# Router of a tiled decoder step: once per four tiles in four column groups instead of once per tile

## The chip, the cores and the metric

The kernel runs on one core of a Trainium2 chip. The metric is the device time of one execution in microseconds (us). The core has a matrix engine (TensorE, PE in the rows, with its weight loads as PEld), a vector engine (DVE), an activation engine (ACT), GpSimd (POOL) and a sync engine (SP), which here only issues DMAs, in order. The engines are tied together by semaphores: an instruction waits until a counter has reached a value, and everything behind it on its engine waits with it.

## What is computed

The reference is one step of a hybrid decoder layer for 2048 prompt tokens and 64 sample tokens of width 1024. Cut to what matters here:

```python
x = x + g1 * (concat(pool_out, ssm_out) @ w_out)
h2 = modulate(rmsnorm(x, norm2_g), sh2, sc2)
lg1 = h2 @ rw1 + rb1                       # 4 columns: the expert groups
lg2 = einsum('td,gde->tge', h2, rw2) + rb2 # 16 columns: the experts
# top-1 group, top-2 experts inside it, gates, then the expert MLPs, gated residual, final norm
```

The ssm half of the mix is g * sigmoid(g @ glu_w + glu_b) (the "GLU"). The router is the product of h2 with the 20 columns of rw1 and rw2.

## The kernel before

The program has the stages front, middle, routing, experts and final_norm, with a barrier between them. The change lies in the second part of `middle`, a loop over 17 tiles: 16 of 128 prompt tokens and a last one (LAST = 16) of 64 sample tokens.

For tile t, in the order that each engine's own list gives:

- **PE**: `product(t, 0)` and `product(t, 1)`, the two column halves of the ssm half of the output projection, each 12 matmuls of 512 columns into `psO[:, t % 2]`; between them `turn(t - 2)`, eight transposes of the rows h2 of tile t-2 into `psH`; behind them `route(t - 2)`, the router; then `gate(t + 5)`, 12 matmuls of the GLU for one of its 20 pieces (`LEAD` is 5, `GLUS` 20; four pieces make one block of four tiles; pieces 16 to 19 are those of the sample tokens and are 64 columns wide).
- **ACT**: sigmoid of the gate, in every fourth tile `g_split` (the high part of the next GLU block), the square sum of the row norm, its square root, `gated_hi`, and `turned(t - 1)`, which copies `psH` to `h2T`.
- **DVE**: `residual(t)` (three passes over 1024 columns: L1706, L1708, L1710), `gated(t + 5)` (L1689), in every fourth tile `g_split`, `mean`, `normed(t)` (L1720, L1721, and L1726, which writes h2), `gated_lo` (L1697), at t = 2 also `scale_rows(1)`, and `logits(t - 2)` (L1731), which adds the bias `rb` to `psR` and writes `lg`.
- **SP**: `store(t)` (x2 to acc_d, L1191, and h2 to h2_d, L1193), then `tile_load(t + 2)` (L1181, L1185: the rows of x and of the pooling half `part_d`), and in tiles 3 and 7 `g_load`, four DMAs of the next GLU block.

Ahead of the loop SP issues, in this order: the broadcast rows g1, a2, sh2 and norm2_g, five DMAs of the router weight `rw` (L1255, L1257), two of the bias `rb` (L1259, L1260), three of the sample tokens' rows, and `g_load(2)` (L1173). The buffers of this part lie over buffers of the first part: `rw`, `rb` and `ss` over `mp_hi`, `h2T` over `ev0`, `n2` over `mraw`.

What ties the router to the rest is this:

```python
def route(t):
    ...
        pe.wait_ge(s["lg_done"], t)      # logits(t - 1) is done on DVE: psR is free
    pe.wait_ge(s["h_ev"], t + 1)         # turned(t) is done on ACT
```

PE's `route(t - 2)` of tile t thus waits for DVE's `logits(t - 3)`, and that is the last thing DVE does for tile t-1. `product(t, 0)` waits for the first pass of `residual(t - 2)`, `gate(n)` for the sigmoid of piece n-1, DVE's `gated(n)` for the sigmoid of piece n, `residual(t)` for `product(t, 1)` and for the landing of `part`.

## Time and profile before

| | |
|---|---|
| median of 3 runs | 1302.78 us (1300.69 to 1307.26) |
| profiled execution | 1300.7 us, its span 1299.0 us |
| PE busy | 1086.8 us, 84% |
| DVE busy | 761.1 us, 59% |
| ACT busy | 512.3 us, 39% |
| mean granted TensorE clock | 0.907 of full speed |

Busy time is the sum over all stages; it doesn't say which engine sets the end in one of them. The rows below are from the span's own clock, which begins with the first instruction. In a timeline row the first number is the start, the second how long the (merged) entry took; in brackets stands the idle time ahead of it and what ended it. A matmul's duration includes its passage through the array, so successive starts, not durations, tell the pace. An fp32 matmul stands as two instructions; the products and gates, in fp32r, as one.

### The profile page before, as it was taken

The numbers are of one execution on the slowest core, as the hardware profiler recorded it, in microseconds if no ns is written. First come the engines' busy times: TensorE is split into PE (matmuls) and PEld (weight loads), VectorE is DVE, ScalarE is ACT, GpSimd is POOL, SyncE is SP. The second block draws the span as 40 slices with busy tenths as digits, with TensorE's granted clock in tenths as the row PEclk, the third lists the DMA queues.
The fourth block names the chain that finished last, engine by engine and source line by source line (L and its number), as shares of the span: only waits on it lengthen the run. The fifth ranks groups of instructions, "written<-read, shape, count | busy, mean of one in ns | idle before, by whom it ended". The sixth has DMA issues, their size and how long they took to land. (4 is left out here: it accounts for less than half of the span.)

```text
span 1299.0 us, 18067 instructions
## 1 busy us (share of the span) xinstructions
PE 1086.8 (84%) x5419; PEld 832.6 (64%) x5420; DVE 761.1 (59%) x1248; ACT 512.3 (39%) x759; POOL 257.1 (20%) x316
## 2 busy tenths in 40 slices
PE   4599999998488989989999824999999999999900
PEld 2266766765265668777788613777787777787700
DVE  2745566630589934475767667465566655555326
ACT  2523333311343225344444321455556545444315
POOL 0035344351140000000000001133233323233200
PEclk9699999998689989988898856999999999999955
DMA  9814646483774458465355453678789778765469
GB/s 295 305 38 123 193 116 196 122 288 98 213 112 131 137 180 259 127 232 162 144 185 195 146 195 120 204 210 224 219 272 284 213 216 223 225 155 108 74 202 394
DMA packets 175876, 244.75 MB, mean 188 GB/s; under 512 B 70903, under 2 KB 131015, under 8 KB 174743
## 3 DMA queue, kind: packets, MB, share of 16 engines
q1 hardware_dynamic: 151049, 180.32, 43.4%
q0 software_dynamic: 12528, 45.62, 15.4%
q10 hardware_dynamic: 12246, 18.14, 4.1%
q8 instruction: 29, 0.48, 0.1%
q14 instruction: 24, 0.20, 0.0%
HBM read 167.80 MB, written 75.84 MB: 188 GB/s over the span
## 5 line engine op out<-in xcount | busy, mean ns | idle before, releaser
L120 PE MATMUL experts_psGU<-weights_we_hi,experts_x_hi 128*128 (+1 forms) x344 | 144.7, 421 | 9.0 <-DVE experts_x_lo L2292 6.9
L121 PE MATMUL experts_psGU<-weights_we_hi,experts_x_lo 128*128 (+1 forms) x344 | 137.5, 400 | 0.0
L122 PE MATMUL experts_psGU<-weights_we_lo,experts_x_hi 128*128 (+1 forms) x344 | 137.5, 400 | 0.0
L120 PE MATMUL front_psM<-front_hT_hi,front_w_hi 128*128 128x512 f32 x256 | 105.7, 413 | 0.0
L2188 POOL DMA_INDIRECT acc_d<-experts_o_sb,experts_to_col x43 | 71.4, 1660 | 149.6 <-issue 64.4
L121 PE MATMUL front_psM<-front_hT_hi,front_w_lo 128*128 128x512 f32 x256 | 100.5, 393 | 0.0
L122 PE MATMUL front_psM<-front_hT_lo,front_w_hi 128*128 128x512 f32 x256 | 100.3, 392 | 0.0
L120 PEld LDWEIGHTS experts_psGU<-weights_we_hi,experts_x_hi 128*128 128x128 f32 x344 | 65.6, 191 | 34.9 <-issue 22.8
L2292 DVE TENSOR_TENSOR experts_x_lo<-experts_psX,experts_x_hi 128x1024 fp32r<-128x1024 f32 x44 | 53.9, 1225 | 45.5 <-ACT experts_x_hi L2224 45.5
L122 PEld LDWEIGHTS experts_psGU<-weights_we_lo,experts_x_hi 128*128 128x128 f32 x344 | 65.6, 191 | 15.7
L121 PEld LDWEIGHTS experts_psGU<-weights_we_hi,experts_x_lo 128*128 128x128 f32 x344 | 65.8, 191 | 12.2
L120 PE MATMUL experts_psD<-weights_wd_hi,experts_hT_hi 128*128 x172 | 71.6, 416 | 1.8 <-DVE experts_hT_lo L2304 1.8
L1939 POOL IOTA routing_io_i<- 128x128 int32 x1 | 0.2, 234 | 367.7 <-POOLq L111 367.7
L2282 DVE TENSOR_TENSOR weights_we_lo<-weights_we_raw,weights_we_hi (+1 forms) x60 | 70.8, 1221 | 0.0
L2298 DVE SCALAR_TENSOR_TENSOR experts_hid<-experts_sg_e,all_gate,experts_psGU 128x256 f32<-128x256 f32 x43 | 20.6, 480 | 84.5 <-ACT experts_sg_e L2230 84.5
L2224 ACT CAST experts_x_hi<-experts_psX 128x1024 fp32r<-128x1024 f32 x44 | 44.7, 1016 | 60.4 <-DMA experts_g<-mod_d 39.4
L122 PE MATMUL experts_psD<-weights_wd_lo,experts_hT_hi 128*128 x172 | 67.9, 395 | 0.0
L121 PE MATMUL experts_psD<-weights_wd_hi,experts_hT_lo 128*128 x172 | 67.9, 395 | 0.0
L2311 DVE TENSOR_TENSOR experts_o_sb<-experts_psD,experts_g2r 128x1024 f32<-128x1024 f32 x43 | 52.7, 1225 | 25.4 <-PE experts_psD L122 25.4
L120 PE MATMUL middle_psO<-middle_wp_hi,middle_mp_hi 128*128 128x512 f32 (+1 forms) x136 | 55.2, 406 | 5.9 <-DVE middle_mp_lo L1639 5.8
L2215 ACT CAST weights_we_hi<-weights_we_raw (+1 forms) x60 | 59.5, 1042 | 0.0
L2349 PE MATMUL experts_psX<-all_ident,weights_xg 128*128 128x128 f32 x352 | 46.5, 276 | 14.5 <-PEq L1935 14.5
(433 smaller groups left out, 2538.0 us busy)
## 6 DMA issues: line engine op xcount, KB each, us to landing
front_raw<-in_w_ada SPq DMA_DIRECT2D x32, 512.0 KB, 4.1
weights_we_raw<-in_exp_w_gate SPq DMA_DIRECT2D x16, 1024.0 KB, 6.0
weights_we_raw<-in_exp_w_up SPq DMA_DIRECT2D x16, 1024.0 KB, 12.5
weights_wd_raw<-in_exp_w_down SPq DMA_DIRECT2D x16, 1024.0 KB, 13.1
front_raw<-in_w_ada SPq DMA_DIRECT2D x8, 1024.0 KB, 11.8
front_xraw<-in_x_prompt SPq DMA_DIRECT2D x4, 2048.0 KB, 10.1
part_d<-middle_ev ACTq DMA_DIRECT2D x16, 512.0 KB, 3.2
middle_xt<-in_x_prompt SPq DMA_DIRECT2D x16, 512.0 KB, 4.8
```

The source lines that it names most:

```text
L120: pe.matmul(out, l_hi, r_hi, start=start, stop=False)
L121: pe.matmul(out, l_lo, r_hi, start=False, stop=False)
L122: return pe.matmul(out, l_hi, r_lo, start=False, stop=stop)
L1939: pool.iota(io_i[:], [[1, P]], base=0, channel_multiplier=0).then_inc(con, 1)
L2188: pool.indirect_dma_start(acc_d, bass.IndirectOffsetOnAxis(tc[:, u, :], 0), osb[:, u, :], None, compute_op=ALU.add).then_inc(added, 16)
L2215: act.copy(w_hi[:, u, q, :], wraw[:, u, q, :]).then_inc(whi, 1)
L2224: act.copy(x_hi[:, u], psX[:].rearrange("p (k n) -> p k n", k=KD)).then_inc(xhi, 1)
L2282: dve.tensor_tensor(w_lo[:, u, q, :], wraw[:, u, q, :], w_hi[:, u, q, :].bitcast(F32), ALU.subtract).then_inc(wlo, 1)
L2292: dve.tensor_tensor(x_lo[:, u], psX[:].rearrange("p (k n) -> p k n", k=KD), x_hi[:, u].bitcast(F32), ALU.subtract).then_inc(xlo, 1)
L2298: dve.scalar_tensor_tensor(out=hid[:, u, :], in0=sg[:], scalar=R.gate[:, bass.ds(t, 1)], in1=psG[:, u, FH:2 * FH], op0=ALU.mult, op1=ALU.m ...
L2311: dve.tensor_tensor(osb[:, u, :], psD[:], g2r[:, u, :], ALU.mult).then_inc(oev, 1)
L2349: mm = pe.transpose(psX[:, q * P:(q + 1) * P], xg[:, u, q * P:(q + 1) * P], k.ident[:])
```

## The change

The router of four tiles becomes one batch. `rw` is now the stationary operand, padded to 32 columns (CR) with zeros, and the turned rows h2T are the moving one; tile j of a batch writes to partitions 32j to 32j+31 of `psR`, so four tiles use four column groups. There are four buffers for h2T. ACT's `route_out` adds the bias, now a column with one value per partition, and writes `lgT`; PE's `turn_logits` transposes the 128x128 result once, and DVE's `logits` copies 4 x 20 columns. `route(b)` stands between `product(t, 0)` and `turn(t - 2)` in tiles 6, 10 and 14; `turn_logits(b)` one tile later. The zeros come from two DVE memsets after DVE's work of the first part, and SP waits for them (`r_zero`) ahead of the router's DMAs. The bias takes eight small DMAs. Five early waits on single DMAs are merged to one semaphore, `smp_in`.

```diff
-        rw = k.over("rw", [P, KD, NR], "mp_hi")
-        rb = k.over("rb", [P, NR], "mp_hi", F32, KD * NR * 4)
-        h2T = k.over("h2T", [P, KD, P], "ev0")
+        late = k.where["mp_hi"]
+        rw = k.at("rw", [P, KD, CR], late)
+        rb = k.at("rb", [P, 1], late + 1024)
+        lgT = k.at("lgT", [P, P], late + 1088)
+        h2T = [k.over("h2T0", [P, KD, P], "ev0"), k.at("h2T1", [P, KD, P], late + 3648),
+               k.at("h2T2", [P, KD, P], late + 3648 + 4096), k.over("h2T3", [P, KD, P], "mraw")]
...
-                sp.dma_start(sprow[:], a["state_pool"][0].rearrange("b j c -> (b j) c")).then_inc(s["sp_in"], 16)
+                sp.dma_start(sprow[:], a["state_pool"][0].rearrange("b j c -> (b j) c")).then_inc(s["smp_in"], 16)
...
+                sp.wait_ge(s["r_zero"], 2)
                 sp.dma_start(rw[:, :, 0:4], a["router_w1"][0].rearrange("(k p) n -> p k n", p=P)).then_inc(s["rw_in"], 16)
...
-                sp.dma_start(rb[:, 0:4], a["router_b1"].broadcast_to([P, 4])).then_inc(s["rw_in"], 16)
-                sp.dma_start(rb[:, 4:NR], a["router_b2"].rearrange("a g e -> a (g e)").broadcast_to([P, NE])
-                             ).then_inc(s["rw_in"], 16)
+                for j in range(TPB):
+                    sp.dma_start(rb[CR * j:CR * j + 4, :], a["router_b1"].rearrange("a n -> n a"),
+                                 allow_slow_non_contiguous=True).then_inc(s["rw_in"], 16)
+                    sp.dma_start(rb[CR * j + 4:CR * j + NR, :], a["router_b2"].rearrange("a g e -> (g e) a"),
+                                 allow_slow_non_contiguous=True).then_inc(s["rw_in"], 16)
...
-                pool.wait_ge(s["zt_in"], 32)
+                pool.wait_ge(s["smp_in"], 112)
...
-                def route(t):
-                    n = rows_of(t)
-                    if t == 0:
-                        pe.wait_ge(s["rw_in"], 16 * 10)
+                def route(b):
+
+                    tiles = range(TPB) if b < NBLK else range(1)
+                    n = rows_of(TPB * b)
+                    if b == 0:
+                        pe.wait_ge(s["rw_in"], 16 * 16)
                     else:
-                        pe.wait_ge(s["lg_done"], t)
-                    pe.wait_ge(s["h_ev"], t + 1)
+                        pe.wait_ge(s["lg_done"], b)
+                    pe.wait_ge(s["h_ev"], TPB * b + len(tiles))
                     for q in range(KD):
-                        mm = pe.matmul(psR[0:n, :], h2T[:, q, 0:n], rw[:, q, :], start=q == 0, stop=q == KD - 1)
+                        for j in tiles:
+                            mm = pe.matmul(psR[CR * j:CR * j + CR, 0:n], rw[:, q, :], h2T[j][:, q, 0:n],
+                                           start=q == 0, stop=q == KD - 1)
                     mm.then_inc(s["r_mm"], 1)
+
+                def turn_logits(b):
+                    r, n = P if b < NBLK else CR, rows_of(TPB * b)
+                    pe.wait_ge(s["r_ev"], b + 1)
+                    pe.transpose(psL[0:n, 0:r], lgT[0:r, 0:n], idt[0:r, 0:r]).then_inc(s["l_t"], 1)
...
                     product(t, 0)
+                    if t >= 6 and t % TPB == 2:
+                        route(t // TPB - 1)
+                    if t >= 7 and t % TPB == 3:
+                        turn_logits(t // TPB - 1)
                     if t >= 2:
                         turn(t - 2)
                     product(t, 1)
-                    if t >= 2:
-                        route(t - 2)
...
-                for t in (LAST - 1, LAST):
-                    turn(t)
-                    route(t)
+                turn(LAST - 1)
+                route(NBLK - 1)
+                turn(LAST)
+                turn_logits(NBLK - 1)
+                route(NBLK)
+                turn_logits(NBLK)
...
+                    if t >= TPB:
+                        act.wait_ge(s["r_mm"], t // TPB)
...
+                def route_out(b):
+                    r, n = P if b < NBLK else CR, rows_of(TPB * b)
+                    act.wait_ge(s["r_mm"], b + 1)
+                    if b:
+                        act.wait_ge(s["l_t"], b)
+                    act.activation(lgT[0:r, 0:n], psR[0:r, 0:n], ACT.Identity, bias=rb[0:r, :]).then_inc(s["r_ev"], 1)
...
+                    if t >= 5 and t % TPB == 1:
+                        route_out(t // TPB - 1)
                     if t:
                         turned(t - 1)
+                    if t == LAST:
+                        route_out(NBLK - 1)
                 turned(LAST)
+                route_out(NBLK)
...
-                def logits(t):
-                    r = slice(0, rows_of(t))
-                    dve.wait_ge(s["r_mm"], t + 1)
-                    tt(lg[r, t, :], psR[r, :], rb[r, :], ALU.add).then_inc(s["lg_done"], 1)
+                def logits(b):
+                    tiles, n = TPB if b < NBLK else 1, rows_of(TPB * b)
+                    dve.wait_ge(s["l_t"], b + 1)
+                    dve.tensor_copy(lg[0:n, TPB * b:TPB * b + tiles, :],
+                                    psL[0:n, 0:CR * tiles].rearrange("p (j n) -> p j n", n=CR)[:, :, 0:NR]
+                                    ).then_inc(s["lg_done"], 1)
...
+                dve.wait_ge(s["p1_mm"], NT)
+                dve.memset(rw[:], 0.0).then_inc(s["r_zero"], 1)
+                dve.memset(rb[:], 0.0).then_inc(s["r_zero"], 1)
                 dve.wait_ge(s["rows_in"], 64)
                 scale_rows(0)
...
-                    if t >= 2:
-                        logits(t - 2)
-                logits(LAST - 1)
-                logits(LAST)
+                    if t >= 6 and t % TPB == 2:
+                        logits(t // TPB - 1)
+                logits(NBLK - 1)
+                logits(NBLK)
```

## Rows read from the trace of the kernel before

**Rows 1.** Waits by who waited for whom, 560 to 720 us (total, times, longest)

```profile
PEld middle_psX L1405 <- DVE front_lg L1731: 12.6, 10, 3.9
```

**Rows 2.** Timeline of PE, tiles 8 to 10 of the loop

```profile
650.75 0.62 PE L120 MATMUL middle_psX<-middle_g_hi,middle_gw_hi 128*128 128x512 f32 x1
...
654.40 0.40 PE L120 MATMUL middle_psO<-middle_ws_hi,middle_m_hi 128*128 128x512 f32 x1
...
661.36 1.96 PE L1405 MATMUL middle_psX<-middle_rw,middle_h2T 128*128 128x20 f32 x16 [0.35 <-DVE front_lg L1731]
```

**Rows 3.** Timeline of DVE, the same tiles

```profile
655.32 1.19 DVE L1689 TENSOR_TENSOR middle_mo<-middle_gf,middle_sg 128x512 f32<-128x512 f32 x1 [3.56 <-ACT middle_sg L1533]
...
661.22 1.22 DVE L1706 TENSOR_TENSOR middle_tmp<-middle_psO,middle_part 128x1024 f32<-128x1024 f32 x1
...
666.95 1.20 DVE L1689 TENSOR_TENSOR middle_mo<-middle_gf,middle_sg 128x512 f32<-128x512 f32 x1 [1.99 <-ACT middle_sg L1533]
```

**Rows 4.** Timeline of DVE, from the end of the first part to tile 2

```profile
538.90 0.69 DVE L1697 TENSOR_TENSOR middle_m_lo<-middle_mo,middle_m_hi 128x512 fp32r<-128x512 f32 x1 [0.69 <-ACT middle_m_hi L1540]
...
543.22 1.23 DVE L1706 TENSOR_TENSOR middle_tmp<-middle_psO,middle_part 128x1024 f32<-128x1024 f32 x1
...
552.96 1.22 DVE L1706 TENSOR_TENSOR middle_tmp<-middle_psO,middle_part 128x1024 f32<-128x1024 f32 x1
...
564.15 1.23 DVE L1706 TENSOR_TENSOR middle_tmp<-middle_psO,middle_part 128x1024 f32<-128x1024 f32 x1 [1.39 <-issue]
```

**Rows 5.** Timeline of PE: the first stage of middle, and gates of tiles 0 and 1

```profile
363.32 0.63 PE L1419 MATMUL middle_psX<-all_ident,middle_sprow 120*128 120x120 f32 x4
...
541.65 0.40 PE L120 MATMUL middle_psX<-middle_g_hi,middle_gw_hi 128*128 128x512 f32 x1
...
550.00 0.40 PE L120 MATMUL middle_psX<-middle_g_hi,middle_gw_hi 128*128 128x512 f32 x1
```

**Rows 6.** Timeline of DVE, tile 2 (with g_split and scale_rows) to tile 3

```profile
569.63 1.21 DVE L1689 TENSOR_TENSOR middle_mo<-middle_gf,middle_sg 128x512 f32<-128x512 f32 x1 [1.73 <-ACT middle_sg L1533]
...
578.66 1.22 DVE L1706 TENSOR_TENSOR middle_tmp<-middle_psO,middle_part 128x1024 f32<-128x1024 f32 x1
```

**Rows 7.** Timeline of DVE, tile 11, whose gate is 64 columns wide

```profile
684.78 1.21 DVE L1706 TENSOR_TENSOR middle_tmp<-middle_psO,middle_part 128x1024 f32<-128x1024 f32 x1
...
694.04 0.17 DVE L1731 TENSOR_TENSOR front_lg<-middle_psX,middle_rb 128x20 f32<-128x20 f32 x1
```

**Rows 8.** Timeline of PE in front: two products in four column groups

```profile
87.25 0.64 PE L503 MATMUL front_psA<-front_raw,front_cT 128*32 128x256 f32 x8
...
113.22 0.63 PE L567 MATMUL front_psX<-front_CLst,front_Bb 64*16 64x128 f32 x16
```

**Rows 9.** Timeline of SP's queue

```profile
345.14 1.61 SPq L1205 DMA_DIRECT2D middle_pscale<-in_pool_scale  x1
...
534.39 8.56 SPq L1257 DMA_DIRECT2D middle_rw<-in_router_w  x4
...
543.61 0.43 SPq L1260 DMA_DIRECT2D middle_rb<-in_router_b  x1
...
546.03 6.92 SPq L1173 DMA_DIRECT2D middle_gf<-g_d  x4
...
558.46 0.38 SPq L1185 DMA_DIRECT2D middle_part<-part_d  x1
...
649.06 5.62 SPq L1173 DMA_DIRECT2D middle_gf<-g_d  x4
```

**Rows 10.** Timeline of DVE, the last tile

```profile
735.24 1.22 DVE L1706 TENSOR_TENSOR middle_tmp<-middle_psO,middle_part 64x1024 f32<-64x1024 f32 x1 [0.16 <-PE middle_psO L122]
...
742.09 1.22 DVE L1726 TENSOR_TENSOR middle_h<-middle_tmp,middle_sh 64x1024 f32<-64x1024 f32 x1
...
750.76 0.17 DVE L1731 TENSOR_TENSOR front_lg<-middle_psX,middle_rb 64x20 f32<-64x20 f32 x1 [3.50 <-PE middle_psX L1405]
```

**Rows 11.** Timeline of PE, the end of middle

```profile
743.44 3.60 PE L1405 MATMUL middle_psX<-middle_rw,middle_h2T 128*128 128x20 f32 x16 [5.43 <-DVE front_lg L1731]
```

More of the change, by code:

```diff
@@ L1108, in middle @@
         n2 = k.over("n2", [P, D], "mraw")
-        rw = k.over("rw", [P, KD, NR], "mp_hi")
-        rb = k.over("rb", [P, NR], "mp_hi", F32, KD * NR * 4)
-        ss = k.over("ss", [P, 2, 4], "mp_hi", F32, KD * NR * 4 + 128)
-        junk = k.over("junk", [P, D], "mp_lo", BF16)
-        h2T = k.over("h2T", [P, KD, P], "ev0")
+        late = k.where["mp_hi"]
+        rw = k.at("rw", [P, KD, CR], late)
+        rb = k.at("rb", [P, 1], late + 1024)
+        ss = k.at("ss", [P, 2, 4], late + 1056)
+        lgT = k.at("lgT", [P, P], late + 1088)
+        junk = k.at("junk", [P, D], late + 1600, BF16)
+        h2T = [k.over("h2T0", [P, KD, P], "ev0"), k.at("h2T1", [P, KD, P], late + 3648),
+               k.at("h2T2", [P, KD, P], late + 3648 + 4096), k.over("h2T3", [P, KD, P], "mraw")]
+        assert late + 3648 + 2 * 4096 <= k.top
         assert k.where["zs"] + 2 * SZ <= k.where["mraw"] and k.where["vt"] + 2 * SZ <= k.where["zs"]
@@ L1118, in middle @@
         psH = psX[:, 0:2, :].rearrange("p a n -> p (a n)")
-        psG, psR = psX[:, 2, :], psX[:, 3, 0:NR]
-        names = ("h0_in", "sp_in", "pw_in", "zt_in", "x_fill", "x_evac", "t_zero", "t_in", "dve_step", "pool_step",
+        psG, psR, psL = psX[:, 2, :], psX[:, 3, 0:P], psX[:, 3, P:2 * P]
+        names = ("smp_in", "x_fill", "x_evac", "t_zero", "t_in", "dve_step", "pool_step",
                  "pooled", "h_ready", "h_head", "np_out", "fin_out", "fin_ok", "zero_out", "wp_in", "wp_h", "wp_l",
@@ L1123, in middle @@
                  "g_mm", "sg_done", "mo_done", "mhi", "mlo", "rows_in", "rw_in", "mm", "tmp",
-                 "x2_done", "sq", "ms", "rt", "h2_done", "h_t", "h_ev", "r_mm", "lg_done")
+                 "x2_done", "sq", "ms", "rt", "h2_done", "h_t", "h_ev", "r_mm", "r_ev", "l_t", "lg_done", "r_zero")
         s = {n: k.sem("m_" + n) for n in names}
@@ L1308, in pooled_product @@
                     if q == 0:
-                        pe.wait_ge(s["pw_in"], 32)
+                        pe.wait_ge(s["smp_in"], 112)
                     pe.wait_ge(s["pooled"], q + 1)
@@ L1414, in _ @@
                         mm.then_inc(s["x_fill"], 1)
-                pe.wait_ge(s["sp_in"], 16)
+                pe.wait_ge(s["smp_in"], 112)
                 x = slot("hist")
@@ L1420, in _ @@
                 mm.then_inc(s["x_fill"], 1)
-                pe.wait_ge(s["h0_in"], 32)
+                pe.wait_ge(s["smp_in"], 112)
                 x = slot("h0")
@@ L1425, in _ @@
                 mm.then_inc(s["x_fill"], 1)
-                pe.wait_ge(s["zt_in"], 32)
+                pe.wait_ge(s["smp_in"], 112)
                 x = slot("np_s")
@@ L1490, in pooled_out @@
                     if q == 0:
-                        act.wait_ge(s["pw_in"], 32)
+                        act.wait_ge(s["smp_in"], 112)
                     if q >= 2:
@@ L1554, in turned @@
                     act.wait_ge(s["h_t"], t + 1)
-                    if t:
-                        act.wait_ge(s["r_mm"], t)
-                    else:
-                        act.wait_ge(part_out[0], 16 * ((NT + 1) // 2))
-                    act.copy(h2T[:, :, 0:n], psH.rearrange("p (k n) -> p k n", k=KD)[:, :, 0:n]).then_inc(s["h_ev"], 1)
+                    if t >= TPB:
+                        act.wait_ge(s["r_mm"], t // TPB)
+                    elif t == 0:
+                        for u in range(2):
+                            act.wait_ge(part_out[u], 16 * ((NT + 1 - u) // 2))
+                    act.copy(h2T[t % TPB][:, :, 0:n], psH.rearrange("p (k n) -> p k n", k=KD)[:, :, 0:n]
+                             ).then_inc(s["h_ev"], 1)
+                def route_out(b):
[4 more added lines that the diff above has]
+                    act.activation(lgT[0:r, 0:n], psR[0:r, 0:n], ACT.Identity, bias=rb[0:r, :]).then_inc(s["r_ev"], 1)
                 for p in range(PAIRS):
@@ L1819, in _ @@
                     if t == 2:
-                        dve.wait_ge(s["rw_in"], 160)
+                        dve.wait_ge(s["rw_in"], 16 * 16)
                         scale_rows(1)
-                    if t >= 2:
-                        logits(t - 2)
-                logits(LAST - 1)
-                logits(LAST)
+                    if t >= 6 and t % TPB == 2:
+                        logits(t // TPB - 1)
+                logits(NBLK - 1)
+                logits(NBLK)
 FQ = FH // P
```

10 lines of the change are left out of this document (5 added, 5 removed).

## The prediction, made before the changed kernel was run

> **What bounds the kernel now.** The shares of busy time (PE 84%, DVE 59%) don't say what sets the pace of the loop over 17 tiles, so I read the waits of that stretch first. The reader should see that PE, the engine with the most work, waits ten times for DVE's bias addition L1731 [rows 1]: `route(t-2)` needs `logits(t-3)`, DVE's last instruction of the tile before. Then come the timelines of PE and DVE over two tiles. DVE begins `gated` at 655.32 and has done everything up to the logits when it begins the next residual at 661.22: 5.90 us. Only then PE starts the router (661.36, idle 0.35 ahead of it), which takes 1.96, then a gate; ACT makes its sigmoid, and the next `gated` starts at 666.95 [rows 2, 3]. The cycle of 5.90 + 5.73 = 11.63 us runs through both engines: DVE idles 1.99 for the sigmoid, PE for the logits. Neither is full. Other tiles take 13.2 us and more, with gate matmuls 0.62 long instead of 0.40 (650.75): the granted clock of those stretches is at its lower level, 1.2 instead of 2.4 GHz. The nine matmuls from 650.75 to 654.40 take 0.41 each [rows 2]; at the upper level it is 0.23, as the gate plus product of 36 matmuls between 541.65 and 550.00 shows, 8.35 us [rows 5].
>
> What would the loop do without that wait? Tiles 0 and 1 show it, since the router isn't in them: DVE starts its residuals at 543.22 and 552.96, a period of **9.74 us**, with nothing in it but DVE's own chain (three residual passes, gated, mean, a round to ACT for the root, normed, m_lo) [rows 4]. PE needs 8.35 for gate and product and about 0.85 for the eight transposes (an estimate: four take 0.63 with their passage through the array [rows 5]): **9.2**. So after the change DVE is the bound, with 0.5 us of slack on PE per tile.
>
> **The change, part by part.**
>
> *The wait and the 17 routers go.* I count DVE's chain from its residual of tile 2 to that of tile 16. Tile 2: g_split and scale_rows make it longer, 578.66 - 569.63 = 9.03 from gated on, plus 3.75 for the residual (three passes at 1.25): 12.8 [rows 6]. Tile 6: the same without scale_rows (1.24): 11.5. Tiles 3, 4, 5, 7, 8, 9: 6 x 9.74 = 58.4. Tile 10, whose g_split is 64 columns wide: 9.9, an estimate. Tiles 11 to 14 have narrow gates: 694.04 + 0.09 - 684.78 = 9.35 each, 37.4 [rows 7]. Tile 15 has no gate: 8.2, as tile 16 shows (735.24 to 743.31 is 8.07) [rows 10]. Sum 138.2. Before, the same way took 735.24 - 564.15 = 171.1 [rows 4, 10]. Gain **32.9 us**.
>
> *The batched router must hide.* It is 64 instructions (32 fp32 matmuls) in tiles 6, 10 and 14. Its form, 32 stationary columns, 128 moving ones, four groups, isn't in this trace; the nearest are 256 moving columns, 8 instructions in 0.64 (at most 80 ns each), and 16 stationary with 64 rows, 16 in 0.63 (39 ns) [rows 8]. Both are far below the 0.12 of a router instruction now (1.96 by 16) [rows 2]. Bounds 39 and 80; I take 50, between them since the columns are those of the second and the rows those of the first: 3.2 us per batch (2.5 to 5.1). PE's lead on DVE covers it: after the cold start of tile 3 (below) I work out that `product(4, 1)` is done some 3.3 us before residual(4) can begin; +0.5 per tile makes 4.3 at tile 6, 1.1 after the router; tile 6's longer DVE chain and the wait for g_split bring it back to some 5 at tile 10, and later tiles win 1.5 each. So nothing shows. Without that cover each batch costs its 3.2.
>
> *A rule of the Trainium skill against it.* In the trace, eight instructions in four groups pass 256 fp32 columns each in 0.64 us [rows 8], less than half the time of 8 x 0.23, the pace at which this trace passes even twice as many fp32r columns one after the other [rows 5]. "TensorE: Matmul & The Clock Gate", Part 3, says that a weight load overlaps matmuls in flight only when the row group differs; column groups all use the same rows, so by it the loads would stand in line and the batch would be nearer its serial price (7.7 us, rival A). The row speaks for overlap.
>
> *ACT and DVE.* `route_out` (128 columns, about 0.3) sits where ACT waits for the transposes; ACT has some 6 of 9.7 us to do. A copy of 80 columns replaces four additions: 0. One transpose, 0.1, in tiles 7, 11 and 15, within PE's slack. I expect no function table to be loaded for Identity; if it were, 1.3 us in ACT's idle time.
>
> *The merged early waits.* The last of the seven DMAs they wait for is issued at 345.14 [rows 9], and PE first needs them at 363.32 [rows 5], behind 128 state products; GpSimd's copy may start later but isn't needed before that either. Cost 0; it would be the landing's delay if it came after 363.
>
> *SP's queue, the part that costs.* The router's DMAs now wait for memsets that stand on DVE behind the m_lo at 538.90 to 539.59 [rows 4]: they can go at about 540.0, where L1257 began at 534.39 [rows 9], with L1255 ahead of it, some 6.3 us later. Those four issues took 8.56 while the broadcast rows filled the DMA engines; later they may take what four DMAs of as many pieces take in a quieter place, 5.62 [rows 9]: delay 3.3 to 6.3, I take 5. The bias takes eight issues instead of two; at 0.43 each (L1260) that is some 2.5 more [rows 9]. Sum **7.5** (5.8 to 9). Queued behind: three sample rows, g_load(2), store(0), tile_load(2). The last of them is what residual(2) waits for already: `part` is issued at 558.46 and residual(2) starts at 564.15, 5.7 later, DVE having been free since 552.96 + 9.74 = 562.7 (its wait of 1.39 has no engine as its cause, so a landing) [rows 4, 9]. So the delay goes one to one into residual(2): about 571.7. The next late one is PE's gate of tile 3 behind g_split: it idles some 10 us, and its clock will be low as it is after such gaps (the router after 5.43 idle takes 3.60 instead of 1.96 [rows 2, 11]); DVE's chain of 12.8 covers this.
>
> *The end.* Now the last logits end 750.93 - 743.31 = 7.6 us after the last h2 [rows 10]. After: ACT copies tile 15 only after the last root, as now; then 64 instructions at the low clock (about 85 ns each, an estimate by the factor of [rows 11], 5.4), last transposes, copy, last router 1.9, and new: route_out, transpose and copy, together 0.8. It begins 1.8 before the last h2 and ends some 8.3 after it: **+0.7** (-1 to +3).
>
> **Sum.** 32.9 - 7.5 - 0.7 = 24.7. The profiled execution took 1300.7; so 1276.0. The median shown is 2.1 above that execution: **1278**.
>
> **The rivals.**
>
> *A, the groups don't run side by side.* A batch costs 64 x 0.12 = 7.7. Over leads of 4.3, 5.3 and 5.5 that is 3.4 + 2.4 + 2.2 = 8, and at the end 64 x 0.22 (3.60 by 16, [rows 11]) = 14 instead of 5.4: +8.6. The gain is 24.7 - 16.6 = 8: **1294**. Against it: [rows 8].
>
> *B, the clock stays low.* If PE falls to 1.2 GHz once per tile as in [rows 2] (a gate 1.6 longer), its period is 10.8 against 9.74, the lead goes, and the batches show: 6 x 1.1 - 3.3 + 2 x 3.2 = 9.7. **1287**. For it: PE still idles in places. Against: in the stretch without the router (541 to 550) no matmul is long [rows 5], and the thin router instructions and the idle ahead of them go.
>
> *C, SP isn't late or catches up.* 32.9 - 0.7 = 32.2: **1270.5**. Against: tile_load(2) was already last.
>
> *D, slower.* The eight bias DMAs address single 4-byte values on separate partitions. If each took long to issue, residual(2) would wait for all: the delay of 5 - 1 + 8x (1 for the two issues of now) exceeds the gain of 32.2 from x = 3.5 us on, and at 5 us the time is about 1302.8 + 11.8 = **1315**. Against it: 0.43 for a bias now, and 1.61 for a DMA of 512 single values [rows 9].
>
> *E, no change.* Another wait of the cycle is as tight as the one removed, so that the tiles keep 11.6 to 13. Against: the period of 9.74 in tiles 0 and 1 contains every other wait [rows 4]. **1303**.
>
> **Chances.** Forecast 0.59, C 0.12, B 0.14, A 0.08, D 0.03, E 0.03, something else slower 0.01. All but D, E and that last one end over 0.5% (6.5 us, about what a measurement tells from no change) faster: 0.93 faster, 0.03 same, 0.04 slower. The range goes from C past B, 1270 to 1290; A, D and E, 0.14 together, stay outside. The forecast's own range, from the bounds of SP's delay, the batch and the end, is 1274 to 1283.
>
> **What would show it.** Right: DVE's residuals of tiles 3 to 5 are 9.7 apart; no wait of PE for L1731; PE's batch about 3 us in tiles 6, 10, 14, with no gap of DVE behind it; DVE idle ahead of residual(2) until about 571.7, with `part` as its cause; middle ends near 726; later stages unchanged. Wrong: periods above 10 with DVE waiting for psO (B, or a batch too long: A), a start of residual(2) far from 571.7 (C, D), or a wait of PE that isn't there now.

## The result and the profile after

The changed kernel takes **1265.65 us** (median of 4 runs, 1262.88 to 1268.91), the kernel before 1302.84 (4 runs, 1300.69 to 1307.26): ratio 0.971, 95% interval 0.968 to 0.975. The gain is 37.2 us where 24.7 was forecast, and the time lies 4 us below the stated range. The profiled execution took 1266.45, against 1300.7 before: 34.3 less.

First the page's busy times after, over all stages.

```profile
span 1264.7 us, 18067 instructions
PE 1050.4 (83%) x5424; PEld 798.6 (63%) x5425; DVE 759.8 (60%) x1238; ACT 513.6 (41%) x764; POOL 261.1 (21%) x316
```

PE is busy for 36 us less (1086.8 before) with as many instructions, and its share hardly moved: the share still says nothing about the pace of this loop. The windows do. Columns: stretch, length, busy time (and count) of PE, PEld, DVE, ACT and POOL, granted clock, DMA share, GB/s. The kernel before, then the one after:

```profile
545.00:700.00 155.00, 145.09 (x699) 120.06 (x698) 104.73 (x124) 73.79 (x99) 0.00 (x0) 0.89 0.55 183
```

```profile
545.00:700.00 155.00, 145.94 (x860) 118.13 (x859) 124.69 (x147) 91.31 (x127) 0.00 (x0) 0.96 0.67 223
```

PE is as busy as before in both, DVE goes from 105 to 125 us of 155, and the clock rises from 0.89 to 0.96. Which engine sets the pace now, the waits of the loop say (after, 575 to 700 us; columns: us in total, times, longest):

```profile
ACT middle_junk L1566 <- DVE middle_xt L1745: 40.3, 12, 5.7
DVE middle_ss L1755 <- ACT middle_ss L1571: 15.5, 13, 1.4
ACT middle_sg L1554 <- PE middle_psX L122: 9.2, 8, 2.6
PEld middle_psO L120 <- issue: 6.1, 5, 3.9
DVE middle_ss L1750 <- ACT middle_junk L1566: 5.9, 8, 1.2
PE middle_psO L120 <- DVE middle_m_lo L1732: 4.8, 2, 3.5
...
```

Ten waits of PE for DVE's bias addition stood here [rows 1]; none is left. ACT waits for DVE. DVE waits for ACT twice in its own chain, for the root (1.36 us in nearly every tile) and, less, for the square sum in front of it (5.9 us in eight waits); for PE it waits once, 0.2 us. So DVE's chain, with its round to ACT, is the bound. Its timeline after, from the last pass of tile 1 on (L1741 is `residual`'s first pass, L1715 `g_split`, L1755 the step behind the root; dots leave out the other rows):

```profile
550.73 1.22 DVE L1741 TENSOR_TENSOR middle_tmp<-middle_psO,middle_part 128x1024 f32<-128x1024 f32 x1
...
563.57 1.22 DVE L1741 TENSOR_TENSOR middle_tmp<-middle_psO,middle_part 128x1024 f32<-128x1024 f32 x1 [3.02 <-issue]
...
568.14 2.29 DVE L1715 TENSOR_TENSOR middle_g_lo<-middle_gf,middle_g_hi 128x2048 fp32r<-128x2048 f32 x1
...
570.76 0.16 DVE L1755 RECIPROCAL middle_ss<-middle_ss 128x1 f32<-128x1 f32 x1 [0.27 <-ACT middle_ss L1571]
...
575.26 1.22 DVE L1741 TENSOR_TENSOR middle_tmp<-middle_psO,middle_part 128x1024 f32<-128x1024 f32 x1
...
581.74 0.16 DVE L1755 RECIPROCAL middle_ss<-middle_ss 128x1 f32<-128x1 f32 x1 [1.36 <-ACT middle_ss L1571]
...
585.00 1.22 DVE L1741 TENSOR_TENSOR middle_tmp<-middle_psO,middle_part 128x1024 f32<-128x1024 f32 x1
...
594.74 1.22 DVE L1741 TENSOR_TENSOR middle_tmp<-middle_psO,middle_part 128x1024 f32<-128x1024 f32 x1
...
604.47 1.22 DVE L1741 TENSOR_TENSOR middle_tmp<-middle_psO,middle_part 128x1024 f32<-128x1024 f32 x1
```

Tiles 3, 4 and 5 take 9.74, 9.74 and 9.73, as tile 0 did before [rows 4]. Tile 2 still waits for a landing, 3.02 us instead of 1.39. The batch and the end on PE (after):

```profile
636.58 1.95 PE L1415 MATMUL middle_psX<-middle_h2T,middle_rw 128*32 128x128 f32 x64
...
706.05 3.64 PE L1415 MATMUL middle_psX<-middle_h2T,middle_rw 128*32 128x128 f32 x64 [5.37 <-ACT middle_h2T L1581]
...
711.09 1.05 PE L1415 MATMUL middle_psX<-middle_h2T,middle_rw 128*32 128x64 f32 x16 [0.51 <-ACT middle_h2T L1581]
```

A batch of 64 instructions takes 1.95 us, 30 ns each: as long as the router of one tile before (1.96, [rows 2]). Behind 5.37 us of idle time it takes 3.64.

**Where the 34.3 us are.** I cut both profiled executions at the same landmarks: start of `middle`, first pass of `residual(0)`, `residual(2)`, `residual(16)`, last h2, last logits, end. The stretch that the table leaves out, `residual(16)` to the last h2, is 6.9 in both.

| stretch | before | after | difference | forecast |
|---|---|---|---|---|
| start to `middle`'s first load | 338.4 | 336.3 | -2.1 | 0 |
| to `residual(0)` | 204.8 | 204.7 | -0.2 | 0 |
| `residual(0)` to `residual(2)` | 20.9 | 22.6 | **+1.7** | +7.5 |
| `residual(2)` to `residual(16)` | 171.1 | 136.1 | **-35.0** | -32.9 |
| last h2 to last logits | 8.7 | 6.3 | **-2.4** | +0.7 |
| last logits to the end | 548.2 | 551.9 | +3.7 | 0 |

The first, second and last row are unchanged code. In another profiled execution of the changed kernel they were 342.0, 204.8 and 544.8: they move by some us each from run to run, so what follows reads the three middle rows, which the change touches. The last column is the prediction's sum by stretch.

### The profile page after: what moved, and what is told of

It is laid out like the page before. It is cut to its first block and busy times, and to the rows that moved or that the text cites. A ratio compares the mean times of both kernels' runs of the same rounds, so it can differ in the third digit from the quotient of the medians.

```text
span 1264.7 us, 18067 instructions
## 1 busy us (share of the span) xinstructions
PE 1050.4 (83%) x5424; PEld 798.6 (63%) x5425; DVE 759.8 (60%) x1238; ACT 513.6 (41%) x764; POOL 261.1 (21%) x316
## 5 line engine op out<-in xcount | busy, mean ns | idle before, releaser
L121 PE MATMUL experts_psGU<-weights_we_hi,experts_x_lo 128*128 (+1 forms) x344 | 137.5, 400 | 0.0
L2228 POOL DMA_INDIRECT acc_d<-experts_o_sb,experts_to_col x43 | 75.5, 1756 | 154.8 <-DMA acc_d<-experts_o_sb,experts_to_col 71.9
L120 PEld LDWEIGHTS experts_psGU<-weights_we_hi,experts_x_hi 128*128 128x128 f32 x344 | 65.7, 191 | 34.5 <-issue 22.6
L2338 DVE SCALAR_TENSOR_TENSOR experts_hid<-experts_sg_e,all_gate,experts_psGU 128x256 f32<-128x256 f32 x43 | 20.7, 480 | 84.6 <-ACT experts_sg_e L2270 84.6
L120 PE MATMUL middle_psO<-middle_ws_hi,middle_m_hi 128*128 128x512 f32 (+1 forms) x136 | 56.6, 416 | 4.8 <-DVE middle_m_lo L1732 4.8
```

Source lines behind the costliest of these rows:

```text
L120: pe.matmul(out, l_hi, r_hi, start=start, stop=False)
L121: pe.matmul(out, l_lo, r_hi, start=False, stop=False)
L2228: pool.indirect_dma_start(acc_d, bass.IndirectOffsetOnAxis(tc[:, u, :], 0), osb[:, u, :], None, compute_op=ALU.add).then_inc(added, 16)
L2338: dve.scalar_tensor_tensor(out=hid[:, u, :], in0=sg[:], scalar=R.gate[:, bass.ds(t, 1)], in1=psG[:, u, FH:2 * FH], op0=ALU.mult, op1=ALU.m ...
```

## The experiments

All twelve, in one table; "before" and "after" are the two kernels given. The ratio is that of a kernel to the kernel before, on the same chip; the landmarks are those of the profiled execution.

| kernel | median | ratio (95%) | r0 to r2 | r2 to r16 | h2 to logits |
|---|---|---|---|---|---|
| before | 1302.8 | 1 | 20.9 | 171.1 | 8.7 |
| after | 1265.7 | 0.971 (0.968 to 0.975) | 22.6 | 136.1 | 6.3 |
| after_again | 1265.2 | 0.970 (0.968 to 0.973) | 23.0 | 136.1 | 6.2 |
| e1_logits_early | 1274.5 | 0.979 (0.977 to 0.981) | 20.7 | 149.9 | 6.8 |
| e2_tile_by_tile | 1274.4 | 0.979 (0.977 to 0.981) | 23.4 | 141.9 | 9.8 |
| e3_zeros_by_gpsimd | 1265.3 | 0.971 (0.969 to 0.973) | 24.2 | 137.3 | 6.4 |
| e4_hold_router_loads | 1301.8 | 0.999 (0.998 to 1.000) | 20.5 | 174.5 | 8.7 |
| e5_router_loads_late | 1267.8 | 0.973 (0.970 to 0.976) | 19.5 | 142.3 | 6.3 |
| e6_add_early | 1270.4 | 0.976 (0.973 to 0.979) | 19.5 | - | 6.5 |
| e7_both | 1271.7 | 0.977 (0.974 to 0.979) | 19.5 | - | 6.3 |
| e8_lo_by_gpsimd | 1269.0 | 0.975 (0.973 to 0.978) | 25.0 | 139.0 | 6.7 |
| e9_loads_split | 1262.0 | 0.968 (0.965 to 0.970) | 19.5 | 137.5 | 6.4 |
| e10_no_root | 1255.4 | 0.964 (0.961 to 0.966) | 24.3 | 128.5 | 6.0 |
| e12_batch_twice | 1267.0 | 0.972 (0.969 to 0.974) | 23.6 | 138.4 | 6.4 |

(e6 and e7 move the first residual pass; from h2 of tile 2 to h2 of tile 16 they take 142.0 and 142.2, the changed kernel 134.3.)

**Is it the wait alone?** The kernel before, with the logits moved into DVE's hole behind `mean`, and no column groups:

```diff
                     mean(t)
+                    if t >= 2:
+                        if t == 2:
+                            dve.wait_ge(s["rw_in"], 160)
+                        logits(t - 2)
                     normed(t)
                     if n < GLUS:
                         gated_lo(n)
                     if t == 2:
-                        dve.wait_ge(s["rw_in"], 160)
                         scale_rows(1)
-                    if t >= 2:
-                        logits(t - 2)
```

> The kernel before, with one move: DVE's logits(t-2) stands right behind mean(t), where DVE waits 1.36 us for ACT's root, instead of at the end of the tile. The router stays one per tile with its 1.8 us on PE. Theory (the wait of PE for DVE's last instruction closes the cycle; PE's own work is the next bound): PE no longer waits for L1731; wide tiles take PE's 9.2 + 1.8 = 11.1 us, residual(2) to residual(16) about 148 instead of 171.1, the end 2 us shorter; in all about 1278, that is some 25 of the 37 us gained by the change, without any column group. Rival (the router's instructions and the low clock that follows them are what costs, not the wait): tiles stay at 12.5 to 13 us with gates at the low clock, 1290 or more.

It takes 1274.5: 28 of the 37 us by the medians, by moving one instruction of 0.2 us. By the landmarks of one profiled execution each it is 23 of 36; the unchanged last stretch alone takes 545.6 in e1's and 551.9 in the changed kernel's. DVE's timeline in e1, where the addition L1731 now lies in the time of the root:

```profile
656.76 0.16 DVE L1715 TENSOR_SCALAR middle_ss<-middle_ss 128x1 f32<-128x1 f32 x1
656.82 0.19 DVE L1731 TENSOR_TENSOR front_lg<-middle_psX,middle_rb 128x20 f32<-128x20 f32 x1
658.25 0.16 DVE L1720 RECIPROCAL middle_ss<-middle_ss 128x1 f32<-128x1 f32 x1 [1.25 <-ACT middle_ss L1550]
```

The clock of 545 to 700 us is 0.96 here too, with all the thin router instructions in it; so it was the wait that cost the clock, not those instructions. What e1 leaves, 149.9 against 136.1, is mostly PE's length: 9.2 us of other work per tile (the prediction's estimate) and the router make 11.1, and seven of its fourteen tiles take 10.7 to 11.3 us where DVE alone would need 9.7 (tiles 3, 4 and 7 do take 9.7, tiles 2 and 6, with `g_split`, 12.9). PE is late there: DVE waits for psO, 3.4 us in 3 waits, and for ACT's sigmoid of a late gate (575 to 700 us):

```profile
DVE middle_mo L1689 <- ACT middle_sg L1533: 7.1, 5, 1.5
```

So the change does two things: it takes the wait away (21 of the 35 us of the loop) and it takes 1.4 us per tile off PE (the other 14), since the batch costs 1.95 per four tiles. The rival, that the wait alone brings little, falls.

**Do the column groups run side by side?** The same 64 instructions in another order, one tile after the other:

```diff
-                    for q in range(KD):
-                        for j in tiles:
+                    for j in tiles:
+                        for q in range(KD):
```

> The changed kernel with the two loops of route(b) swapped: all eight products of tile 0 in its column group, then those of tile 1, and so on, so that neighbours in the queue share a column group. Theory (a batch is short, 1.95 us for 64 instructions, because neighbours lie in different column groups and overlap): a batch now takes 6 to 8 us in tiles 6, 10 and 14; PE's lead covers most of it there (DVE waits for psO by 0 to 3 us each), and the last batch, at the low clock and uncovered, grows from 3.6 to 10 or more; in all +8 to +16 us. Rival (it is the narrow stationary operand of 32 columns that makes them short): a batch stays at 2 to 3 us and the time within 1 us of the changed kernel's.

```profile
598.09 5.96 PE L1415 MATMUL middle_psX<-middle_h2T,middle_rw 128*32 128x128 f32 x64
...
641.04 5.95 PE L1415 MATMUL middle_psX<-middle_h2T,middle_rw 128*32 128x128 f32 x64
```

5.96 against 1.95 us, a factor of 3.06, from the order alone. So neighbours in different column groups overlap, and neighbours in the same one pass at 93 ns each. (The order also decides whether neighbours add into the same rows of psR; no run keeps the two apart, and for the order of the loops it makes no difference.) 9 us go: 5.7 in the loop (r2 to r16; DVE waits for psO again, 5.0 us in 3 waits), 3.6 at the end, where the last batch takes 7.2 (713.32 to 720.54) and not the 10 or more that I expected. "TensorE: Matmul & The Clock Gate" of the Trainium skill (Part 3) has weight loads overlap only when the row group differs. All 64 instructions use the same rows, so by it both orders would cost the same; the runs differ threefold, and the measurement decides. The same page of the Trainium skill has in its table a factor of 2.38 for three column tiles with 512 moving columns; no run here has that form, four with 128 columns give 3.06.

**How much of a batch is hidden?** Every batch but the last issued twice:

```diff
-                    for q in range(KD):
-                        for j in tiles:
+                    for _ in range(2 if b < NBLK - 1 else 1):
+                        for q in range(KD):
+                            for j in tiles:
...
```

> The changed kernel with each of the batches in tiles 6, 10 and 14 issued twice, 1.95 us more of PE each; the one at the end stays single. Theory (they lie in PE's lead over DVE, 4 us or more ahead of each): residual(2) to residual(16) and the total unchanged within 1 us. Rival (they are on the path): 4 to 6 us longer.

```profile
602.65 3.70 PE L1416 MATMUL middle_psX<-middle_h2T,middle_rw 128*32 128x128 f32 x128
```

128 instructions take 3.70 (29 ns each). r2 to r16 is 2.3 longer, more than the 1 us expected, but 1.2 of that is the last period (9.5 instead of 8.3), where DVE waits 1.4 us for PE; that wait also stands in e3 and e9, which leave the batches alone. What is left is 1.0, in tiles 5, 6 and 9, for 5.3 us of added PE work: four fifths hidden, about as the lead of 4 to 5 us in the prediction would have it.

**SP's queue, the term that was wrong.** The kernel before, with the router's DMAs held back to where the change puts them:

```diff
+                sp.wait_ge(s["mlo"], LEAD)
                 sp.dma_start(rw[:, :, 0:4], a["router_w1"]...
```

> The kernel before, with the router's DMAs held back on SP until DVE's gated_lo(4) has ended, as the changed kernel holds them, and nothing else. Theory (as for the run with GpSimd): the four issues shrink from 8.56 to about 3 us, SP is where it was, residual(2) and the total unchanged within 1.5 us. Rival (my prediction's price of 3.3 to 6.3 us for the held-back queue): residual(2) starts 3 to 6 us later and the total rises by as much.

Nothing: 0.999, and r0 to r2 is 20.5 as before (20.9). Its r2 to r16 is 3.4 longer than that of the one profiled execution before, mostly by tiles 9, 13 and 14, which its median doesn't show: the old loop varies by this much, and so do the 35.0 above and e1's 21. SP's rows:

```profile
539.59 0.38 SPq L1256 DMA_DIRECT2D middle_rw<-in_router_w  x1
540.02 3.31 SPq L1258 DMA_DIRECT2D middle_rw<-in_router_w  x4
543.37 0.58 SPq L1260 DMA_DIRECT2D middle_rb<-in_router_b  x1
543.99 0.43 SPq L1261 DMA_DIRECT2D middle_rb<-in_router_b  x1
...
546.41 6.86 SPq L1173 DMA_DIRECT2D middle_gf<-g_d  x4
```

The four issues begin 5.6 us later than in [rows 9] and end at 543.3, only 0.4 later than there (534.39 + 8.56 = 542.95). The changed kernel shows the same, and then its eight bias issues:

```profile
537.71 0.38 SPq L1260 DMA_DIRECT2D middle_rw<-in_router_w  x1
538.13 2.85 SPq L1262 DMA_DIRECT2D middle_rw<-in_router_w  x4
541.03 0.49 SPq L1265 DMA_DIRECT2D middle_rb<-in_router_b  x1
...
543.74 0.31 SPq L1267 DMA_DIRECT2D middle_rb<-in_router_b  x1
...
546.06 6.39 SPq L1177 DMA_DIRECT2D middle_gf<-g_d  x4
...
557.76 0.38 SPq L1189 DMA_DIRECT2D middle_part<-part_d  x1
```

The other way round: the changed kernel, with the zeros written by GpSimd, so that SP needn't wait for DVE.

```diff
-                dve.wait_ge(s["p1_mm"], NT)
-                dve.memset(rw[:], 0.0).then_inc(s["r_zero"], 1)
-                dve.memset(rb[:], 0.0).then_inc(s["r_zero"], 1)
...
+                pool.wait_ge(s["p1_mm"], NT)
+                pool.memset(rw[:], 0.0).then_inc(s["r_zero"], 1)
+                pool.memset(rb[:], 0.0).then_inc(s["r_zero"], 1)
```

> The changed kernel with the two memsets of rw and rb on GpSimd right behind the wait for the first part, instead of on DVE behind gated_lo(4): SP can issue the router's DMAs some 6 us earlier, directly behind the broadcast rows. Theory (those issues go no faster than the DMA engines work off the rows ahead of them): the four DMAs of L1262 take 7 to 9 us again instead of 2.85, SP reaches the sample rows within 1.5 us of where it does now, residual(2) starts within 1 us of now, total within 1.5 us. Rival (SP's wait for the zeros is a real delay, as I had predicted): residual(2) starts 1.5 to 3 us earlier relative to residual(0), as early as DVE is free, and the total falls by as much.

```profile
534.01 8.43 SPq L1262 DMA_DIRECT2D middle_rw<-in_router_w  x4
542.48 0.48 SPq L1265 DMA_DIRECT2D middle_rb<-in_router_b  x1
```

Issued early, the four take 8.43 again and end at 542.4; issued after the wait, 2.85. The time is that of the changed kernel (1265.3), though residual(2) comes 24.2 behind residual(0), 1.2 to 1.6 later than in the changed kernel's two profiled executions and not within the 1 us expected. In e5 below, the four DMAs of `g_load(2)` stand right behind the broadcast rows: they take 9.16, and 6.39 in their place in the changed kernel. So most of 8.56 was waiting until the DMAs ahead had moved on, and holding the four back merely replaced one wait by another. What the change costs on SP is the bias: eight issues in 3.0 us (541.03 to 544.05) where two took 1.1 (e4's rows, 543.37 to 544.42), **2.0 us**. (That these 2.0 are what makes residual(2) later is argued from the rows; no run takes the eight issues away alone.)

**Could the rest of SP's cost be had back?** The changed kernel, with the router's five DMAs, the bias's eight and the three sample rows (`router_loads`, taken from above `g_load(2)`) behind `store(0)` and `tile_load(2)`, and `scale_rows(1)` at tile 3:

```diff
...
                     if t + 2 < NT:
                         tile_load(t + 2)
+                    if t == 0:
+                        router_loads()
...
-                    if t == 2:
+                    if t == 3:
                         dve.wait_ge(s["rw_in"], 16 * 16)
```

> The changed kernel with the router's DMAs, the eight of the bias and the three sample rows moved on SP behind store(0) and tile_load(2), and scale_rows(1) on DVE moved from tile 2 to tile 3, so that nothing waits for them earlier. Theory (residual(2) waits for the landing of part, which stands behind these loads in SP's queue): residual(2) starts when DVE is free, 19.5 us after residual(0) instead of 22.6; total 2 to 4 us shorter, about 1262.5. Rival (the DMA engines, not the queue, set the landing, since the same bytes move): residual(2) at most 1 us earlier, total unchanged.

Tile 2 is no longer late (19.5 = 2 x 9.74), but tile 3 is, by 6.0 us, and the median is no better (the theory's 1262.5 failed):

```profile
581.93 1.23 DVE L1745 TENSOR_TENSOR middle_tmp<-middle_psO,middle_part 128x1024 f32<-128x1024 f32 x1 [6.03 <-issue]
```

SP was busy with the moved issues up to 568.05, so the store of tile 1's x2 came late, and with it the loads into the same buffer:

```profile
567.43 0.57 SPq L1271 DMA_DIRECT2D middle_sh<-mod_d  x1
568.05 0.45 SPq L1195 DMA_DIRECT2D acc_d<-middle_xt  x1
...
575.77 0.34 SPq L1185 DMA_DIRECT2D middle_xt<-in_x_prompt  x1
576.21 0.38 SPq L1189 DMA_DIRECT2D middle_part<-part_d  x1
```

A split avoids that. `part(t + 2)` goes right behind the store of x2 (its buffer is free already, only x's is not), the weights behind tile 0's entries and the bias and sample rows behind tile 1's:

```diff
+                def part_load(t):
+                    u, n = t % 2, rows_of(t)
+                    sp.wait_ge(part_out[u], 16 * (t // 2 + 1))
+                    if t >= 2:
+                        sp.wait_ge(s["tmp"], t - 1)
+                    sp.dma_start(part[0:n, u, :], part_d[t * P:t * P + n, :]).then_inc(part_in[u], 16)
...
                     sp.dma_start(x2, xt[0:n, u, :]).then_inc(xt_out[u], 16)
+                    if t + 2 < NT:
+                        part_load(t + 2)
...
+                    if t == 0:
+                        weight_loads()
+                    if t == 1:
+                        row_loads()
```

> The changed kernel with SP's queue in another order: part(t+2) is issued right behind the store of x2(t), the router's five weight DMAs stand behind tile 0's entries, the bias and sample rows behind tile 1's, and scale_rows(1) on DVE in tile 3. Theory (what cost tile 3 its 6 us when all of these loads stood behind tile_load(2) was that part(3) came after them): residual(2) starts 19.5 us after residual(0), tiles 2 and 3 take 10.5 and 11 us, the rest 9.7; in all 2 to 4 us below the changed kernel of the same job. Rival (the many small pieces of these loads delay whatever stands behind them in the queue, wherever they stand): the 3 us come back as a wait in tile 3 or 4, total within 1 us.

r0 to r2 is 19.5 and tiles 2 and 3 take 10.6 and 11.0: **1262.0**, the fastest complete kernel here, 3.2 below the changed kernel run beside it on the same chip (1265.2; the intervals of the ratios, 0.9651 to 0.9698 and 0.9678 to 0.9726, still overlap by 0.002, so the gain is likely rather than shown). Most of what residual(2) gains may come from `part_load` alone: e6 below has it too, with the router's loads where the change puts them, and its residual(2) starts at 19.5 as well and waits only 0.84 us, for x. In the changed kernel `part(2)` stands behind SP's wait for the landing of `store(0)` (SP issues nothing between 553.86 and 557.32). No run has `part_load` as its only edit. Of the changed kernel, run once more, this was expected:

> The changed kernel once more, beside the runs that vary it by less than 1%: 1263 to 1268, residual(2) 22 to 24.5 us after residual(0), residual(16) 136 to 137.5 us after residual(2).

**Is DVE the bound of the changed loop?** The changed kernel without ACT's square root, DVE taking the reciprocal of the mean square itself; the root and its share in h2 are left out of the computation.

```diff
-                    root(t)
...
-                    dve.wait_ge(s["rt"], t + 1)
-                    ch.link(dve.reciprocal(ss[r, u, 3:4], ss[r, u, 2:3]))
+                    dve.wait_ge(s["ms"], t + 1)
+                    ch.link(dve.reciprocal(ss[r, u, 3:4], ss[r, u, 1:2]))
```

> The changed kernel without ACT's square root: DVE takes the reciprocal of the mean square itself, so that the norm is left out in part and the values of h2 differ. With it go ACT's two table loads per tile and DVE's wait of 1.36 us for the root. Theory (DVE's chain bounds the changed loop, PE's 9.2 us per wide tile stands right behind it): wide tiles fall from 9.74 to PE's 9.2 to 9.4, narrow ones from 9.3 to 7.9 to 8.1, residual(2) to residual(16) 6 to 10 us shorter. Rival (PE and DVE wait in turn at the start of each block, as in the run with the early sum): less than 3 us shorter, with DVE waiting for psO in most tiles.

```profile
592.77 1.22 DVE L1735 TENSOR_TENSOR middle_tmp<-middle_psO,middle_part 128x1024 f32<-128x1024 f32 x1
...
597.72 0.15 DVE L1744 TENSOR_SCALAR middle_ss<-middle_ss 128x1 f32<-128x1 f32 x1
597.91 0.16 DVE L1749 RECIPROCAL middle_ss<-middle_ss 128x1 f32<-128x1 f32 x1
```

Taking 1.36 us of waiting out of DVE's chain brings the ordinary tiles from 9.7 to 8.4 and r2 to r16 down by 7.6: DVE's chain did set the pace. It isn't 14 x 1.36 = 19: in tiles 2 and 6 `g_split` hid most of the root already (0.27 of waiting in each), and PE is next: DVE then waits for psO, 6.9 us in 4 waits, where the changed kernel has none over 0.2.

**Can DVE's chain be made shorter without leaving anything out?** Three tries, all slower by the median than the changed kernel (1269.0 to 1271.7 against 1265.2 to 1265.7, on different chips; the interval of each still touches one of the changed kernel's two). First, the first residual pass of the next tile put into the hole of the root, and, so that its operand is there, `part_load` as in e9:

```diff
...
                     mean(t)
+                    if 2 <= t < LAST:
+                        add_halves(t + 1)
                     normed(t)
```

> The changed kernel with the first pass of residual(t+1), the sum of psO and part, done by DVE right behind mean(t) from tile 2 on, in the 1.36 us in which it waits for ACT's root, and with SP issuing part(t+2) ahead of the store of h2. Theory (DVE's chain of 9.74 us per tile is the bound; PE's 9.2 stands right behind it): wide tiles fall from 9.74 to PE's 9.2 to 9.3, narrow ones from 9.3 to about 8.1, the batches of the router (1.95 us on PE) begin to show; residual(2) to residual(16) 5 to 9 us shorter than the 136.1 of the changed kernel, total about 1259. Rival (the loop is bound by PE and DVE taking turns, so that an earlier sum waits for PE): DVE waits for psO instead, less than 2 us gained or something lost.

```profile
DVE middle_tmp L1748 <- PE middle_psO L122: 21.5, 9, 5.7
...
PE middle_psO L120 <- DVE middle_m_lo L1739: 9.1, 3, 4.3
```

(575 to 700 us.) DVE now needs psO half a tile earlier, 4.4 us, and PE can't have it by then. At a block's start the product waits for that block's last m_lo, which DVE itself writes a tile earlier; that is three of the waits, and DVE waits for psO nine times, so the rest isn't explained by it and stays open. The hole is filled and a greater one opened. With e5's router loads beside it, it is no better; neither gain adds:

> The edits of the two runs before together. Theory (they act in different places, one ahead of residual(2), one behind it): the gains add, 8 to 12 us below the changed kernel, about 1256. Rival: PE, which idles ahead of residual(2) and builds its lead there, loses that lead; the sum is 3 us or more short of the two gains.

Then `gated_lo` on GpSimd, from piece 5 on:

```diff
-                    if n < GLUS:
-                        gated_lo(n)
...
+                for n in range(LEAD, GLUS):
...
+                    pool.wait_ge(s["mhi"], n + 1)
...
+                    pool.tensor_tensor(m_lo[b % 2][:, m, 0:w], mo[:, n % 2, 0:w],
+                                       m_hi[b % 2][:, m, 0:w].bitcast(F32), ALU.subtract).then_inc(s["mlo"], 1)
```

> The changed kernel with gated_lo of pieces 5 to 19 (L1732, 0.6 us of DVE's chain in a wide tile) on GpSimd, which is idle there. Theory (DVE's chain is the bound): wide tiles fall by up to 0.5 us to PE's 9.2, total 3 to 5 us shorter, if GpSimd's pass (128 x 512, by the 1.5 us of its 128 x 176 some 4 to 5 us) doesn't slow DVE's own. Rival (the two share a path to memory): DVE's passes of 1.22 us grow beside it, and the total is equal or higher.

```profile
596.47 2.20 DVE L1770 TENSOR_TENSOR middle_h<-middle_tmp,middle_sh 128x1024 f32<-128x1024 f32 x1
```

```profile
595.50 2.08 POOL L1310 TENSOR_TENSOR middle_m_lo<-middle_mo,middle_m_hi 128x512 fp32r<-128x512 f32 x1 [8.02 <-ACT middle_m_hi L1570]
```

DVE saves a pass of 0.6 and loses 1.0 on the one beside GpSimd's, 2.20 instead of 1.22: the tile takes 10.1 instead of 9.7. GpSimd's pass takes 2.08, not the 4 to 5 us expected. "GPSIMD Engine Reference" of the Trainium skill (section 1, Specifications) says that GpSimd shares its SBUF interfaces with VectorE and contends with instructions of two SBUF inputs; that pass has two, and the trace agrees.

## Why the prediction was right in sign and 12.5 us short

By its own steps, in the order of its sum; the working is above.

- **The wait goes, and DVE becomes the bound: right, and shown** (e1, e10, and the waits after). The chain was 138.2, measured 136.1. Tiles 3 to 5 and 7 to 9 hit to 0.1 us. Tile 2 was priced 12.8 and took 11.69, tile 6 11.5 and took 10.66. I had taken the length from a tile [rows 6] in which the gate came late, so that DVE also waited for ACT's high part of the next block. The root isn't the difference, it costs 0.27 in both. Before:

```profile
571.42 2.29 DVE L1680 TENSOR_TENSOR middle_g_lo<-middle_gf,middle_g_hi 128x2048 fp32r<-128x2048 f32 x1 [0.59 <-ACT middle_g_hi L1525]
...
574.04 0.16 DVE L1720 RECIPROCAL middle_ss<-middle_ss 128x1 f32<-128x1 f32 x1 [0.27 <-ACT middle_ss L1550]
```

  From the start of `gated` to that of `g_split` it is 1.79 there (569.63 to 571.42) and 0.91 after (567.23 to 568.14, no wait between): 0.9 of the 1.1, the old addition of the logits another 0.1. **2.1 us** of the miss, over all tiles.
- **SP's queue, 7.5: this is the step that failed.** The prediction says "Those four issues took 8.56 while the broadcast rows filled the DMA engines; later they may take what four DMAs of as many pieces take in a quieter place, 5.62 [rows 9]: delay 3.3 to 6.3, I take 5." It names why they took 8.56 and doesn't draw the conclusion: time spent waiting for the queue ahead isn't added to a later start, it is used up by it. They took 2.85 and ended, counted from residual(0), 0.3 us later than before. So of the 5 for the four issues nothing is left, and of the 2.5 for the bias 2.0. Measured in all: 1.7 us between r0 and r2 (residual(2) starts at 563.57, forecast 571.7), 1.7 to 3.4 over six profiled executions with the change's order of DMAs, 4.1 in e8, whose tiles are longer. **5.9 us** of the miss. Rival C, SP not late, was nearest to what happened, at 0.12.
- **The batch.** Priced 50 ns per instruction, between bounds of 39 and 80; it is 30, below the lower bound. In the loop this cost the forecast nothing, since it was hidden at either price (e12: twice the batch, 3.70, shows 1.0 us in three tiles). With the loops the other way round (e2) the batch is as serial as the rule has it: 5.96 (I had 7.7), and the time is 1274. So rival A's mechanism exists, only not in this order, and it costs 9 us where A had 16.6.
- **The end, +0.7, was -2.4.** Two prices: the cold batch 5.4, measured 3.64, and the last router 1.9, carried over from before, measured 1.05 with the operands swapped. These are 2.6 of the **3.1 us**; the rest is in the waits between them.
- **The clock.** Rival B had it stay low; 0.96 instead of 0.89 refutes it. The cold start of tile 3 is there, behind 4.2 us of idle time (some 10 in the forecast, since `residual(2)` was thought to come later): gate matmuls after it start 0.43 apart, the pace of the lower clock level, 1.2 GHz, where they start 0.23 apart at the upper one.

```profile
570.58 0.77 PE L120 MATMUL middle_psX<-middle_g_hi,middle_gw_hi 128*128 128x512 f32 x1 [4.22 <-DVE middle_g_lo L1715]
571.14 0.63 PE L121 MATMUL middle_psX<-middle_g_hi,middle_gw_lo 128*128 128x512 f32 x1
571.57 0.63 PE L122 MATMUL middle_psX<-middle_g_lo,middle_gw_hi 128*128 128x512 f32 x1
```

- **ACT and the merged waits at nothing: right.** `route_out` takes 0.36 with no table load for it, and `middle` reaches `residual(0)` in 204.7 as before.
- **The rest.** 5.9 + 3.1 + 2.1 = 11.1 of the 12.5. Unchanged code took 1.4 us more in the profiled execution after, and the medians stand 2.1 above the profiled execution before and 0.8 below the one after, 2.9 together; both are variation between runs, and I have no cause for them. 11.1 - 1.4 + 2.9 = 12.6. The shares are those of one pair of profiled executions; with the other executions SP's part would be 4.1 to 5.9.

The range missed for the same reason: its lower end was rival C with every other term at its central value, and the end and the chain both came out below theirs. The bounds of the batch's price (39 ns) hadn't held the truth either.

What stays open: why `residual(16)` waits 1.4 us for PE in e3, e9 and e12 and 0.2 in the changed kernel. It is worth 1.2 us, and no run was made for it.

## What to carry to other kernels

Ask of a wait not only what it costs but where the waited-for instruction stands: a pass of 0.2 us at the end of an engine's tile cost more here (21 us) than the length of the matmuls it held up (14), and moving it into a hole was worth two thirds (by the landmarks) to three quarters (by the medians) of the whole redesign. A long issue time in a queue may be a wait for the queue ahead; if so, starting it later is free as long as that wait would have lasted (here 5.6 us), and what costs is the number of issues added. When a batch in column groups is written, the loop over the groups belongs inside.

## What the runs showed of the hardware

- 64 fp32 instructions (32 stationary columns, 128 moving ones, four column groups) take 1.95 us when neighbours use different groups and 5.96 when they use the same; 128 of them take 3.70. Behind 5.4 us of idle time 64 take 3.64.
- The same four DMA issues take 8.56, 8.43, 3.31, 2.85, 5.08 or 5.79 us by where they stand in the stream (before, e3, e4, after, e9, e5). The four of `g_load(2)` take 6.39 behind the router's, 9.16 right behind the broadcast rows (after, e5).
- A DMA of single 4-byte values on separate partitions takes 0.31 to 0.49 us to issue in the changed kernel (in e9 up to 0.82); the bias as broadcast rows took 0.43 and 0.58.
- A DVE pass over 128x1024 with two operands in SBUF takes 2.20 us beside a GpSimd pass over 128x512, and 1.22 alone; GpSimd's takes 2.08, DVE's own of that size 0.69.
